# Experts' stage: best 16 sought among 64 sums, marks in fp16, one-hots in one pass, dots paced beside U, one return a tile

## Chip, cores and metric

The kernel runs on one core of a Trainium2 chip. The metric is the device time of one execution in microseconds. Five engines work side by side and are synchronised by semaphores only: TensorE (PE, with its weight loads as PEld), VectorE (DVE), ScalarE (ACT), GpSimd (POOL) and SyncE (SP), which here does nothing but issue DMAs. Each runs its own instructions strictly in order.

## What is computed

A first block (attention, a state-space layer, and a mixture of experts with product keys), then two hybrid layers with feed-forward parts, over 512 tokens of width 1024 in fp32. The change touches the mixture of experts alone:

```python
q = (hc @ w_query).reshape(T, 8, 256)                        # 8 heads
s1 = einsum('chd,hkd->chk', q[..., :128], keys1)             # 128 keys a half
s2 = einsum('chd,hkd->chk', q[..., 128:], keys2)
v1, i1 = top_k(s1, 16);  v2, i2 = top_k(s2, 16)
cand = (v1[..., :, None] + v2[..., None, :]).reshape(T, 8, 256)
sc, ci = top_k(cand, 16)
idx = take(i1, ci // 16) * 128 + take(i2, ci % 16)           # one of 16384 experts
g = softmax(sc)
act = gelu(einsum('chkd,cd->chk', peer_u[idx], hc)) * g
out = einsum('chk,chkd->cd', act, peer_v[idx])
```

## The kernel before

The 512 tokens are four tiles of 128, one token a partition. Tiles 0 to 2 (384 tokens) are computed densely: all 16384 experts, 128 U tiles of 128 experts each, then 128 V tiles; the gates, mostly zero, decide what counts. Tile 3 (`GATHERED`) is computed by gathering: 128 picks (8 heads x 16), for each one row of U and one of V per token, 512 KB a pick.

Each fp32 weight tile (512 KB) is loaded into one of three raw buffers, rounded by ScalarE to fp32r (L338) and its remainder taken by VectorE (L348, "split"); three products (L357 to L359, high x high, high x low, low x high) make one fp32 product. `split_ve` and `split_ac` run up to four tiles ahead of TensorE.

- `pe_u`, `ac_u`, `ve_u`, `sp_u` go through 144 items: 16 query tiles `("wq", c)` and 128 `("U", j)`. A U item is 24 matmuls of 384 columns; ScalarE takes the Gelu of the result (L2021) into one of three buffers, and SP stores it to DRAM (`sp_act`, "acts", 192 KB).
- Beside them, VectorE picks: `ve_top` (best 16 of 128), `ve_cand` (the 16 x 16 sums of a head), `ve_best` (best 16 of 256, five operations of `ve_top16`), `ve_places` (row and column from the place), `ve_mark` (looks up the index by a comparison with 0..15, a product and a sum), `ve_index` (rows to gather). Then `ve_gate`: for 8 tokens at a time, one-hot matrices of both indices in fp16, the second times the gate as two fp16 parts; TensorE multiplies them (`pe_gate`, 16 matmuls of 128 columns), ScalarE copies the result out, and each four groups SP stores 2 MB of gates.
- GpSimd gathers with an indirect DMA (L2081), first the 128 rows of U, then those of V, into five row buffers in turn. `ve_dot` (L2152) multiplies and sums a U row, `ve_row` (L2175) adds a weighted V row to one of two accumulators.
- In V, step j is 18 matmuls of 512 columns into six banks held to the end (`pe_v`). Its left side is acts x gates: SP brings back acts (`sp_back`, 192 KB a tile, six buffers) and gates (`sp_gc`, 768 KB for four tiles, pieces of 512 bytes), VectorE multiplies (L2324), ScalarE rounds (AH, L2316), VectorE takes the remainder (AL, L2326): `ve_prep`/`ac_prep`, `LEAD` = 3 tiles ahead of TensorE.
- The last four V tiles (`TAIL`) are done token tile by token tile, so that the next stage's norm can start: before tile i's last product TensorE does the turn (transpose) of a finished tile, `self.next.pe_turn(order[i])`, and order is 3, 0, 1, 2.

The order is written out by `Peer.schedule`: it goes through the items with a time budget for VectorE (4.4 us for a query item, 3.0 for a U item, 0.8 more with a gate) and puts in units with assumed costs until it is used up; dots fill what is left from four items after the index is known. `later` does the same for V with 1.78 us a step. At the end of U, at item `loads0`, SP issues both first gate returns and the first six acts in one batch.

Of the kernel before, what the change touches and what calls it, by code (L numbers as in the profile page):

```python
# [1824 lines left out]
class Peer:  # L1825
    def __init__(self, k):
# [6 lines left out]
        self.I1T, self.I2T = ar(TOKENS, dt=HF), ar(TOKENS, dt=HF)  # L1833
        self.GP = ar(2, TOKENS, dt=HF)
# [7 lines left out]
        self.IOI = ar(16).bitcast(I32)  # L1842
        self.IOF = ar(16)
        self.KT = ar(16, 128)
        self.V12 = ar(4, 8, 2, 16)
        self.IX = ar(4, 8, 2, 16)
        self.SC, self.CI, self.CJ = ar(4, 8, 16), ar(4, 8, 16), ar(4, 8, 16)
        self.IXu, self.CIu, self.CJu = (x.bitcast(U32) for x in (self.IX, self.CI, self.CJ))
# [7 lines left out]
        self.MK = ar(8, 16, 16)  # L1856
        self.CA = self.KT.rearrange("p a b -> p (a b)").rearrange("p (h k) -> p h k", k=256)
# [5 lines left out]
        self.O1 = [ar(4, 128, 2, dt=HF) for _ in range(4)]  # L1863
        self.O2 = ar(4, 128, 2, dt=HF)
        self.RH = [ar(2, 4, 128, 2, dt=HF) for _ in range(4)]
# [9 lines left out]
    ROWS, SCORES, CHUNK = 5, 8, 32  # L1875
# [5 lines left out]
    def schedule(self):  # L1881
        units = [("top", c, i) for c in range(16) for i in range(4)] + [("rows",)]
        for i in (GATHERED, 0, 1, 2):
# [5 lines left out]
        cost = {"top": 1.7, "rows": 1.3, "cand": 2.5, "best": 2.4, "places": 2.5, "soft": 0.8, "mark": 7.0,  # L1889
                "index": 0.3, "norm": 2.1, "turned": 3.5, "gate": 2.9, "dot": 1.3}  # L1890
        self.items = [("wq", c) for c in range(16)] + [("U", j) for j in range(128)]
        self.units = [[] for _ in self.items]
        self.extras = [[] for _ in range(len(self.items) + 1)]
        time, turn, known, dots = 0.0, None, None, 0
        for n, (kind, c) in enumerate(self.items):
            time = min(time, 2.0) + (4.4 if kind == "wq" else 3.0)
            while time > 0:
                u = units[0] if units else ("dot", dots)
                wait = u[0] == "top" and n < u[1] + 2 or u[0] == "turned" and n < turn + 2
                if wait or u[0] == "gate" and self.units[n] and ("gate", u[1] - 1) in self.units[n]:  # L1900
                    u = ("dot", dots)
                if u[0] == "dot" and (known is None or n < known + 4 or dots == PICKS):
                    break
                time -= cost[u[0]]
                if u[0] == "gate":
                    time += 0.8
                    self.extras[n + 1].append(u)
                if u[0] == "norm":
                    turn = n
                    self.extras[n + 1].append(("turn",))  # L1910
                if u[0] == "soft":
                    self.extras[n].append(u)
                if u[0] == "index":
                    known = n
                if u[0] == "dot":
                    dots += 1
                    if dots % self.CHUNK == 0:
                        self.extras[n + 1].append(("gelu", dots // self.CHUNK - 1))
                    self.units[n].append(u)
                else:  # L1920
                    self.units[n].append(units.pop(0))
        assert not units
        gates = [n for n, x in enumerate(self.extras) if any(u[0] in ("turn", "gate") for u in x)]
        self.loads0 = max(gates) + 4
        assert self.loads0 < len(self.items) - 1, self.loads0


        later = [("dot", x) for x in range(dots, PICKS)] + [("act", c) for c in range(PICKS // self.CHUNK)]
        later += [("row", x) for x in range(PICKS)]
        self.later, self.gelus, time, gelu = [[] for _ in range(128)], [[] for _ in range(128)], 0.0, 0  # L1930
        for j in range(128):
            time = min(time, 1.0) + 1.78
            while later and time > 0:
                u = later[0]
                if u[0] == "act" and u[1] == PICKS // self.CHUNK - 1 and j < gelu + 2:
# [6 lines left out]
        self.later[127] += later  # L1942

# [45 lines left out]
    def pe_gate(self, n, t):  # L1989
# [6 lines left out]
        for c in range(2):  # L1996
            last = pe.e.matmul(self.gate_bank[:, 128 * (t % 4):128 * (t % 4) + 128],
                               self.O1[n % 4][:, t // 2, :, t % 2], self.RH[n % 4][:, c, t // 2, :, t % 2],
# [4 lines left out]
    def ac_u(self):  # L2003
        k, ac, at = self.k, self.k.ac, self.k.at
        a = ac.e.activation
        for n, (kind, c) in enumerate(self.items):
# [16 lines left out]
            for x in self.extras[n]:  # L2023
# [38 lines left out]
    def po_u(self):  # L2062
# [5 lines left out]
        po.after().tensor_copy(self.IOX, bc(self.IO, 2, 2))  # L2068
        g.iota(self.IOI, pattern=[[1, 16]], base=0, channel_multiplier=0).then_inc(*po.up())
        po.after().tensor_copy(self.IOF, self.IOI).then_inc(*po.up("iota"))  # L2070
# [14 lines left out]
    def ve_u(self):  # L2085
# [3 lines left out]
                "gate": self.ve_gate, "rows": self.ve_rows, "index": self.ve_index, "dot": self.ve_dot}  # L2089
# [12 lines left out]
    def ve_cand(self, i):  # L2102
        k, ve, at = self.k, self.k.ve, self.k.at

        ve.wait_ge(*at("ps", 15))
        a = bc(self.V12[:, i, :, 0, :], 3, 16)
        b = bc(self.V12[:, i, :, 1, :], 2, 16)
        ve.after().tensor_tensor(self.CA.rearrange("p h (a b) -> p h a b", b=16), a, b, ALU.add).then_inc(*ve.up())

    def ve_best(self, i, h):  # L2110
        ve_top16(self.k, self.CA[:, h, :], self.SC[:, i, h, :], self.CIu[:, i, h, :],
                 self.TMP).then_inc(*self.k.ve.up())

    def ve_places(self, i):

        k, ve, v, at = self.k, self.k.ve, self.k.ve.e, self.k.at
        ve.wait_ge(*at("iota"))
        ve.after().tensor_copy(self.IX[:, i], self.IXu[:, i]).then_inc(*ve.up())
        v.tensor_scalar(self.CJu[:, i], self.CIu[:, i], 15, None, ALU.bitwise_and).then_inc(*ve.up())
        ve.after().tensor_copy(self.CJ[:, i], self.CJu[:, i])  # L2120
        v.tensor_scalar(self.CIu[:, i], self.CIu[:, i], 4, None, ALU.logical_shift_right).then_inc(*ve.up())
        ve.after().tensor_copy(self.CI[:, i], self.CIu[:, i]).then_inc(*ve.up())

    def ve_mark(self, i, half):

        ve, MK = self.k.ve, self.MK
        sel, dst = ((self.CI, self.E1), (self.CJ, self.E2))[half]
        ve.after().tensor_tensor(MK, bc(sel[:, i, :, :], 3, 16), bc(bc(self.IOF, 1, 16), 1, 8),
                                 ALU.is_equal).then_inc(*ve.up())
        ve.after().tensor_tensor(MK, MK, bc(self.IX[:, i, :, half, :], 2, 16), ALU.mult).then_inc(*ve.up())  # L2130
        ve.after().tensor_reduce(dst[:, i, :, :], MK, AX, ALU.add).then_inc(*ve.up())
# [62 lines left out]
    def ve_turned(self):  # L2194
        k, ve, v, at = self.k, self.k.ve, self.k.ve.e, self.k.at
        GT, GR = (x[:, 0:TOKENS] for x in self.QT)
        for n, dst in enumerate((self.I1T, self.I2T)):
            ve.wait_ge(*at("peT", n))
            v.tensor_copy(dst, k.got("peT", n)[:, 0:TOKENS]).then_inc(*ve.free(("peT", n)))
        ve.wait_ge(*at("peT", 2))  # L2200
        v.tensor_scalar(GT, k.got("peT", 2)[:, 0:TOKENS], GSCALE, None, ALU.mult).then_inc(*ve.free(("peT", 2)))
        ve.after().tensor_copy(self.GP[:, 0, :], GT).then_inc(*ve.up())
        ve.after().tensor_tensor(GR, GT, self.GP[:, 0, :], ALU.subtract).then_inc(*ve.up())
        ve.after().tensor_copy(self.GP[:, 1, :], GR).then_inc(*ve.up())
        k.end("pick", ve)

    def ve_gate(self, n):
        k, ve, v, at = self.k, self.k.ve, self.k.ve.e, self.k.at
        o1, o2, rh = self.O1[n % 4], self.O2, self.RH[n % 4]
        s = slice(8 * n, 8 * n + 8)  # L2210

        def pairs(x):
            return bc(x[:, s].rearrange("p (t u) -> p t u", u=2), 2, 128)

        io = bc(self.IOX, 1, 4)
        if n == 0:
            k.begin(ve, "pick", "ve")
# [9 lines left out]
        last.then_inc(*ve.up("rh", n))  # L2227

    def sp_u(self):
        k, sp, at = self.k, self.k.sp, self.k.at  # L2230
        groups = self.GATES // 4
        for n, item in enumerate(self.items):
# [9 lines left out]
            if n == self.loads0:  # L2242

                sp.wait_ge(*at("gstore", groups - 2))
                sp.wait_ge(*at("gstore", groups - 1))
                sp.wait_ge(*at("pg", self.GATES - 1, 1))
                for c in range(2):
                    self.sp_gc(c)
                for j in range(self.BACK):
                    self.sp_back(j)  # L2250
# [26 lines left out]
    def pe_v(self):  # L2277
        k, pe, at = self.k, self.k.pe, self.k.at
        ps = {(i, n): k.open(2 * i + n, 2 * i + n + 1, "py", i, n) for i in range(DENSE) for n in range(2)}

        def one(j, i, n, w):
            a, c = slice(128 * i, 128 * i + 128), slice(512 * n, 512 * n + 512)
# [3 lines left out]
        for j in range(TAIL):  # L2286
# [3 lines left out]
            for i in range(DENSE):  # L2290
# [37 lines left out]
    def ac_v(self):  # L2328
        k, ac, at = self.k, self.k.ac, self.k.at
        for j in range(self.LEAD):  # L2330
            self.ac_prep(j)
# [11 lines left out]
    def ve_v(self):  # L2343
        k, ve, v, at = self.k, self.k.ve, self.k.ve.e, self.k.at
        does = {"dot": self.ve_dot, "act": self.ve_act, "row": self.ve_row}
        for j in range(self.LEAD):
            self.ve_prep(j)
# [1612 lines left out]
```

## Time and profile before

| | us |
|---|---|
| three runs, median | 4060.3 |
| three runs, lowest and highest | 4057.35, 4067.49 |
| profiled execution, span from first to last instruction | 4053.1 |
| TensorE busy in it | 3751.7 (93%) |
| VectorE busy | 2368.8 (58%) |
| ScalarE busy | 1349.2 (33%) |
| GpSimd busy | 555.0 (14%) |

The page cuts the span into 40 slices of 101 us, in tenths of busy time; the experts' stage is about slices 4 to 17:

```profile
PE   9789999999799999499999788999999999689999
DVE  5746899888688888733237764332333266943332
POOL 8600000111444444300000000000000000100000
PEclk9779999999899999799999879999999999799999
DMA  3003465688999999633322102333222221012222
```

How to read the rows further down. A window's row has start and end, its length, then for each engine busy us and, in brackets, how many instructions; then the granted TensorE clock (1.00 is full speed), the mean busy share of the 16 DMA engines, and GB/s. A row in order of time has its start, its duration, engine, line, operation, what is written and read with shapes, and in square brackets how long the engine was idle before it and what released it. Two instructions of one engine overlap a little: start to start is less than a duration. A group's row has line, engine, operation, forms and count, then busy us and mean ns, then idle time before. A DMA's row ends with KB, where known, and the median us from issue to landing.

### The profile page before, as it was taken

To read this page: it belongs to the slowest core of one execution; us is meant where nothing else is said; L and a number is where in the kernel's file an instruction comes from. 1 tells how busy PE (TensorE), PEld (TensorE's weight loads), DVE (VectorE), ACT (ScalarE), POOL (GpSimd) and SP (SyncE) were. 2 spreads that over 40 slices of the span, in tenths; PEclk is the share of its full clock that TensorE was granted. 3 is DMA by queue.
4 is the path that set the end of the run, shared out by engine and by line. 5 is a ranking of instruction groups with operands and counts; after the bars stand their busy time and mean duration, and the time that the engine had idled before them with its cause. 6 is when DMAs were issued, how large, how long until landed. Compare 5 with 4: busy or idle time off the path is not lost. (4 is left out here: it accounts for less than half of the span.)

```text
span 4053.1 us, 46458 instructions
## 1 busy us (share of the span) xinstructions
PE 3751.7 (93%) x18298; PEld 3094.6 (76%) x18298; DVE 2368.8 (58%) x4034; ACT 1349.2 (33%) x2352; POOL 555.0 (14%) x612
## 2 busy tenths in 40 slices
PE   9789999999799999499999788999999999689999
PEld 7667999988677777378787667887887877467877
DVE  5746899888688888733237764332333266943332
ACT  3354333444233333232233334222322233333221
POOL 8600000111444444300000000000000000100000
PEclk9779999999899999799999879999999999799999
DMA  3003465688999999633322102333222221012222
GB/s 123 11 27 89 126 198 170 237 301 302 348 349 352 347 356 351 242 97 96 98 74 73 44 1 79 94 94 96 81 94 94 95 77 53 19 42 78 95 98 73
DMA packets 273433, 574.70 MB, mean 142 GB/s; under 512 B 19952, under 2 KB 159376, under 8 KB 271552
## 3 DMA queue, kind: packets, MB, share of 16 engines
q1 hardware_dynamic: 236256, 437.42, 33.0%
q0 software_dynamic: 36864, 134.23, 9.1%
q8 instruction: 145, 2.38, 0.2%
q14 instruction: 72, 0.59, 0.0%
q10 hardware_dynamic: 96, 0.08, 0.0%
HBM read 517.92 MB, written 53.74 MB: 141 GB/s over the span
## 5 line engine op out<-in xcount | busy, mean ns | idle before, releaser
L348 DVE TENSOR_TENSOR wlast<-wraw,wlast 128x1024 fp32r<-128x1024 f32 x406 | 494.8, 1224 | 498.1 <-ACT wlast L338 497.5
L357 PE MATMUL ps<-XH,wlast 128*128 128x512 f32 (+2 forms) x1888 | 722.0, 382 | 17.6 <-ACT arena L2021 17.6
L359 PE MATMUL ps<-XH,wlast 128*128 128x512 f32 (+2 forms) x1888 | 706.9, 374 | 0.0
L358 PE MATMUL ps<-XL,wlast 128*128 128x512 f32 (+2 forms) x1888 | 706.8, 374 | 0.0
L338 ACT ACTIVATE wlast<-wraw 128x1024 fp32r<-128x1024 f32 x406 | 425.0, 1052 | 248.4 <-PE ps L359 231.5
L348 DVE TENSOR_TENSOR wtwo<-wraw,wtwo 128x1024 fp32r<-128x1024 f32 x212 | 259.5, 1226 | 302.9 <-ACT wtwo L338 302.5
L357 PEld LDWEIGHTS ps<-XH,wlast 128*128 128x128 f32 x1888 | 357.4, 189 | 77.5 <-ACT arena L2021 18.3
L358 PEld LDWEIGHTS ps<-XL,wlast 128*128 128x128 f32 x1888 | 357.8, 189 | 54.6
L359 PEld LDWEIGHTS ps<-XH,wlast 128*128 128x128 f32 x1888 | 356.8, 189 | 55.5
L357 PE MATMUL ps<-XH,wtwo 128*128 128x512 f32 (+1 forms) x960 | 368.0, 383 | 0.3 <-ACT arena L2021 0.3
L358 PE MATMUL ps<-XL,wtwo 128*128 128x512 f32 (+1 forms) x960 | 361.2, 376 | 0.0
L359 PE MATMUL ps<-XH,wtwo 128*128 128x512 f32 (+1 forms) x960 | 361.2, 376 | 0.0
L2081 POOL DMA_INDIRECT arena<-in_u,arena x128 | 175.1, 1368 | 766.1 <-DVE arena L2152 528.4
L338 ACT ACTIVATE wtwo<-wraw 128x1024 fp32r<-128x1024 f32 x212 | 222.9, 1052 | 160.3 <-PE ps L359 155.8
L357 PE MATMUL ps<-wlast,AH 128*128 128x512 f32 x504 | 202.0, 401 | 31.8 <-DVE AL L2326 31.7
L2081 POOL DMA_INDIRECT arena<-in_v,arena x128 | 190.8, 1490 | 210.2 <-DVE X L2175 98.2
L3096 POOL TENSOR_SCALAR_AFFINE_SELECT arena<-arena 128x128 f32<-128x128 f32 x6 | 3.7, 614 | 1484.3 <-DVE arena L3117 1484.3
L357 PEld LDWEIGHTS ps<-XH,wtwo 128*128 128x128 f32 x960 | 182.4, 190 | 28.8 <-ACT arena L2021 0.7
L358 PEld LDWEIGHTS ps<-XL,wtwo 128*128 128x128 f32 x960 | 182.7, 190 | 28.3
L359 PEld LDWEIGHTS ps<-XH,wtwo 128*128 128x128 f32 x960 | 182.4, 190 | 28.6
L2508 DVE TENSOR_TENSOR arena<-arena,ps 128x512 f32<-128x512 f32 x88 | 60.6, 688 | 245.6 <-PE ps L359 245.6
L2316 ACT ACTIVATE AH<-arena 128x384 fp32r<-128x384 f32 x128 | 67.2, 525 | 398.9 <-DVE arena L2324 398.9
(489 smaller groups left out, 7016.3 us busy)
## 6 DMA issues: line engine op xcount, KB each, us to landing
wraw<-in_ut SPq DMA_DIRECT2D x128, 512.0 KB, 4.2
wraw<-in_v SPq DMA_DIRECT2D x128, 512.0 KB, 6.7
wraw<-in_ffn_gate SPq DMA_DIRECT2D x88, 512.0 KB, 3.5
wraw<-in_ffn_up SPq DMA_DIRECT2D x88, 512.0 KB, 3.5
wraw<-in_ffn_down SPq DMA_DIRECT2D x88, 512.0 KB, 3.5
wraw<-in_w_in SPq DMA_DIRECT2D x58, 512.0 KB, 3.7
acts<-arena SPq DMA_DIRECT2D x128, 192.0 KB, 4.7
gates<-arena SPq DMA_DIRECT2D x12, 2048.0 KB, 10.4
```

The costliest lines, as they stand in the source:

```text
L338: ac.e.activation(W.items[n][7], W.rawof(n), ACT.Copy).then_inc(*ac.up("whi", n))
L348: ve.e.tensor_tensor(W.items[n][8], W.rawof(n), W.items[n][7], ALU.subtract).then_inc(*ve.up("wlo", n))
L357: mm(out, lh, rh, start=start, stop=False)
L358: mm(out, lh, rl, start=False, stop=False)
L359: return mm(out, ll, rh, start=False, stop=stop)
L2081: g.indirect_dma_start(out=self.RB[n % self.ROWS], out_offset=None, in_=tables[n // PICKS], in_offset=bass.IndirectOffsetOnAxis(ap=self.PL ...
L2316: ac.e.activation(self.AH[:, j % 6, :], self.AI[j % 6], ACT.Copy).then_inc(*ac.up("ah", j))
L2508: v.tensor_tensor(s, s, k.got((*id, "up", f)), ALU.mult).then_inc(*ve.free(((*id, "up", f),)))
L3096: po.e.affine_select(out=s, in_=s, compare_op=ALU.is_ge, fill=NEG, base=0, pattern=[[-1, 128]], channel_multiplier=1).then_inc(*po.up("cau ...
```

## The change

- `ve_cand` forms 64 of the 256 sums, in four operations: row 0 with all 16 columns, rows 1 to 3 with 8, rows 4 to 7 with 4, rows 8 to 15 with column 0. All places (a, b) with (a+1)(b+1) at most 16 are among them. `ve_best` searches 64.
- `ve_places` gets row A and column B back from a place in this list, with minima and maxima in fp16, and doubles the indices into pairs (`PAIR`).
- `ve_mark` works in fp16: comparison and product over 2048 elements, then four adds that halve the length instead of one reduction.
- `ve_gate` makes both one-hots in one comparison (2048 elements) and both parts of the gates in one product; three buffers of each instead of four. `ve_turned` lays indices and gates out for that.
- `schedule` has new costs, sets at least one dot an item (`PACE`) from four items after the index is known, spreads the returns as one an item from two items after the last gate, puts the first three `prep`s into the last three U items, and fits what is left evenly into 118 V steps.
- `pe_v` opens the banks as they are first used, takes token tiles in the order 1, 2, 0, and in the tail puts the turn of the gathered tile behind tile 0, with tile 0's own ahead of tile 1's last product.
- Two small constants of GpSimd (`IOI`, `IOF`) go.

Cut to its core:

```diff
-        cost = {"top": 1.7, "rows": 1.3, "cand": 2.5, "best": 2.4, "places": 2.5, "soft": 0.8, "mark": 7.0,
-                "index": 0.3, "norm": 2.1, "turned": 3.5, "gate": 2.9, "dot": 1.3}
+        cost = {"top": 1.7, "rows": 1.3, "cand": 1.0, "best": 1.35, "places": 2.8, "soft": 0.8, "mark": 4.1,
+                "index": 0.3, "norm": 2.1, "turned": 3.5, "gate": 2.5, "dot": 1.35}
...
+            if n > last - self.LEAD:
+                self.units[n].append(("prep", n - last + self.LEAD - 1))
+                self.extras[n].append(("prep", n - last + self.LEAD - 1))
+                time -= 1.2
             while time > 0:
...
+                if known is not None and dots < (n - known - 4) * self.PACE:
+                    u = ("dot", dots)
...
-        self.loads0 = max(gates) + 4
+        back = [("gates", 0)] + [("act", j) for j in range(self.BACK)]
+        back[4:4] = [("gates", 1)]
+        for m, x in enumerate(back):
+            self.returns[min(gates + 2 + m, last)].append(x)
...
+        pace = (first * 1.3 + PICKS * 1.28) / 118
         for j in range(128):
-            time = min(time, 1.0) + 1.78
+            time = min(time, 1.0) + pace
...
     def ve_cand(self, i):
+        ve.after().tensor_tensor(CA[:, :, 0:16], a[:, :, 0:1].broadcast_to([128, 8, 16]), b, ALU.add)
+        v.tensor_tensor(CA[:, :, 16:40].rearrange("p h (a b) -> p h a b", b=8), bc(a[:, :, 1:4], 3, 8),
+                        bc(b[:, :, 0:8], 2, 3), ALU.add)
...
     def ve_mark(self, i, half):
-        ve.after().tensor_reduce(dst[:, i, :, :], MK, AX, ALU.add).then_inc(*ve.up())
+        for n in (8, 4, 2):
+            ve.after().tensor_tensor(MK[:, :, 0:n, :], MK[:, :, 0:n, :], MK[:, :, n:2 * n, :],
+                                     ALU.add).then_inc(*ve.up())
...
     def ve_gate(self, n):
-        v.tensor_tensor(o2, io, pairs(self.I2T), ALU.is_equal).then_inc(*ve.up("o2", n))
-        v.tensor_tensor(o1, io, pairs(self.I1T), ALU.is_equal)
-        ve.wait_ge(*at("o2", n))
-        for c in range(2):
-            last = v.tensor_tensor(rh[:, c], o2, pairs(self.GP[:, c]), ALU.mult)
+        v.tensor_tensor(o.rearrange("p c t i u -> p (c t) i u"), bc(self.IOX, 1, 8), pairs(self.I12),
+                        ALU.is_equal).then_inc(*ve.up("o", n))
+        ve.wait_ge(*at("o", n))
+        v.tensor_tensor(rh.rearrange("p c t i u -> p c t (i u)").rearrange("p c t (i u) -> p c t i u", u=2),
+                        bc(o[:, 1], 1, 2), pairs(self.GP).rearrange("p (c t) i u -> p c t i u", c=2),
+                        ALU.mult).then_inc(*ve.up("rh", n))
...
     def sp_u(self):
-            if n == self.loads0:
+            for x in self.returns[n]:
+                if x == ("gates", 0):
                     sp.wait_ge(*at("gstore", groups - 2))
                     sp.wait_ge(*at("gstore", groups - 1))
...
     def pe_v(self):
-            for i in range(DENSE):
+            for i in (1, 2, 0):
...
-                if j == 127:
+                if j == 127 and i:
+                    if i == 1:
+                        self.next.pe_turn(self.next.order[0])
                     self.next.pe_turn(self.next.order[i])
```

## Rows read from the trace of the kernel before

**Rows 1.** Windows: us, busy (count) of PE PEld DVE ACT POOL; PEclk, DMA, GB/s

```profile
459.00:1040.00 581.00, 579.43 (x3746) 547.87 (x3744) 502.48 (x922) 225.87 (x345) 61.10 (x55) 1.00 0.73 243
1040.00:1072.00 32.00, 10.40 (x50) 9.87 (x48) 15.56 (x25) 5.33 (x8) 15.06 (x10) 0.71 0.92 321
1072.00:1657.00 585.00, 540.99 (x2250) 425.11 (x2250) 475.70 (x621) 185.48 (x254) 267.23 (x173) 0.98 0.98 350
...
1100.00:1130.00 30.00, 30.00 (x131) 24.42 (x130) 25.86 (x42) 10.22 (x14) 15.69 (x10) 1.00 0.97 343
...
1657.00:1704.00 47.00, 3.52 (x17) 3.54 (x17) 34.41 (x33) 5.84 (x13) 22.46 (x21) 0.50 0.75 261
```

**Rows 2.** VectorE in order of time, one V step: start, us, operation, idle before

```profile
1636.26 0.56 DVE L2326 TENSOR_TENSOR AL<-arena,AH 128x384 fp32r<-128x384 f32 x1 [0.59 <-ACT AH L2316]
1636.73 1.28 DVE L2175 SCALAR_TENSOR_TENSOR arena<-arena 128x1024 f32<-128x1024 f32 x1
1637.93 1.22 DVE L348 TENSOR_TENSOR wlast<-wraw,wlast 128x1024 fp32r<-128x1024 f32 x1
1639.06 0.55 DVE L2324 TENSOR_TENSOR arena<-arena 128x384 f32<-128x384 f32 x1
1640.21 0.56 DVE L2326 TENSOR_TENSOR AL<-arena,AH 128x384 fp32r<-128x384 f32 x1 [0.59 <-ACT AH L2316]
```

**Rows 3.** VectorE's waits in V, 1072 to 1657: us, times, longest

```profile
DVE AL L2326 <- ACT AH L2316: 74.5, 126, 0.6
DVE arena L2324 <- DMA arena<-acts: 32.9, 21, 3.1
```

**Rows 4.** VectorE's groups by form, 345 to 1030; the gathers' DMAs, 760 to 1000

```profile
L2152 DVE CUSTOM_DVE_ANT_0 arena<-arena 128x1024 f32<-128x1024 f32 x46 | 55.9, 1221 | 6.9 <-DMA arena<-in_u,arena 6.9
...
L2130 DVE TENSOR_TENSOR arena<-arena 128x2048 f32<-128x2048 f32 x8 | 18.3, 2294 | 0.3
...
L1799 DVE MAX8 arena<-arena 128x8 f32<-128x256 f32 x32 | 13.7, 428 | 1.1
...
L1799 DVE MAX8 arena<-arena 128x8 f32<-128x128 f32 x64 | 18.9, 295 | 3.3
...
L2226 DVE TENSOR_TENSOR arena<-arena 128x1024 f16<-128x1024 f16 x96 | 61.8, 685 | 0.0
...
arena<-in_u,arena POOLq DMA_INDIRECT x31, 5.4
```

**Rows 5.** TensorE in order of time at V's end and the next stage's start

```profile
1656.23 0.63 PE L359 MATMUL ps<-wtwo,AL 128*128 128x512 f32 x1
1700.48 3.75 PE L558 MATMUL ps<-arena,X 128*128 128x128 f32 x16 [43.63 <-DVE arena L590]
...
1726.81 0.77 PE L357 MATMUL ps<-XH,wlast 128*128 128x512 f32 x1
```

**Rows 6.** VectorE in order of time: of the last rows, one and the last

```profile
1668.50 1.29 DVE L2175 SCALAR_TENSOR_TENSOR arena<-arena 128x1024 f32<-128x1024 f32 x1 [2.43 <-DMA arena<-in_v,arena]
...
1695.85 1.28 DVE L2175 SCALAR_TENSOR_TENSOR arena<-arena 128x1024 f32<-128x1024 f32 x1
```

**Rows 7.** ScalarE in order of time: Gelu of U tiles, without and with gates

```profile
563.71 0.49 ACT L2021 ACTIVATE arena<-ps 128x384 f32<-128x384 f32 x1 [2.79 <-PE ps L359]
...
567.95 0.49 ACT L2021 ACTIVATE arena<-ps 128x384 f32<-128x384 f32 x1 [2.80 <-PE ps L359]
...
843.65 0.49 ACT L2021 ACTIVATE arena<-ps 128x384 f32<-128x384 f32 x1 [2.97 <-PE ps L359]
...
849.01 0.49 ACT L2021 ACTIVATE arena<-ps 128x384 f32<-128x384 f32 x1 [2.95 <-PE ps L359]
```

**Rows 8.** Hand-over: SP's DMA queue, ScalarE in order of time, one window

```profile
1034.59 9.91 SPq L2271 DMA_DIRECT2D arena<-acts  x6
...
1056.36 0.49 ACT L2021 ACTIVATE arena<-ps 128x384 f32<-128x384 f32 x1 [19.70 <-DMA acts<-arena]
...
1050.00:1055.00 5.00, 0.00 (x0) 0.00 (x0) 0.00 (x0) 0.00 (x0) 0.00 (x0) 0.50 1.04 400
```

More of the change, by code:

```diff
@@ L1862, in __init__ @@
         self.GS = [ar(128, 32) for _ in range(2)]
-        self.O1 = [ar(4, 128, 2, dt=HF) for _ in range(4)]
-        self.O2 = ar(4, 128, 2, dt=HF)
-        self.RH = [ar(2, 4, 128, 2, dt=HF) for _ in range(4)]
+        self.O = [ar(2, 4, 128, 2, dt=HF) for _ in range(self.AHEAD)]
+        self.RH = [ar(2, 4, 128, 2, dt=HF) for _ in range(self.AHEAD)]
         k.close()
@@ L1888, in schedule @@
         units += [("norm",), ("turned",)] + [("gate", n) for n in range(self.GATES)]
-        cost = {"top": 1.7, "rows": 1.3, "cand": 2.5, "best": 2.4, "places": 2.5, "soft": 0.8, "mark": 7.0,
-                "index": 0.3, "norm": 2.1, "turned": 3.5, "gate": 2.9, "dot": 1.3}
+        cost = {"top": 1.7, "rows": 1.3, "cand": 1.0, "best": 1.35, "places": 2.8, "soft": 0.8, "mark": 4.1,
+                "index": 0.3, "norm": 2.1, "turned": 3.5, "gate": 2.5, "dot": 1.35}
         self.items = [("wq", c) for c in range(16)] + [("U", j) for j in range(128)]
+        last = len(self.items) - 1
         self.units = [[] for _ in self.items]
         self.extras = [[] for _ in range(len(self.items) + 1)]
-        time, turn, known, dots = 0.0, None, None, 0
+        self.returns = [[] for _ in self.items]
+        time, turn, known, dots, gates = 0.0, None, None, 0, None
         for n, (kind, c) in enumerate(self.items):
             time = min(time, 2.0) + (4.4 if kind == "wq" else 3.0)
+            if n > last - self.LEAD:
+                self.units[n].append(("prep", n - last + self.LEAD - 1))
+                self.extras[n].append(("prep", n - last + self.LEAD - 1))
+                time -= 1.2
             while time > 0:
@@ L1907, in schedule @@
                     self.extras[n + 1].append(u)
+                    gates = n + 1
                 if u[0] == "norm":
@@ L1922, in schedule @@
         assert not units
-        gates = [n for n, x in enumerate(self.extras) if any(u[0] in ("turn", "gate") for u in x)]
-        self.loads0 = max(gates) + 4
-        assert self.loads0 < len(self.items) - 1, self.loads0
-        later = [("dot", x) for x in range(dots, PICKS)] + [("act", c) for c in range(PICKS // self.CHUNK)]
+        back = [("gates", 0)] + [("act", j) for j in range(self.BACK)]
+        back[4:4] = [("gates", 1)]
+        for m, x in enumerate(back):
+            self.returns[min(gates + 2 + m, last)].append(x)
+        assert gates + 2 + 3 <= last - self.LEAD, gates
+        later = [("dot", x) for x in range(dots, PICKS)]
+        first = len(later)
+        later += [("act", c) for c in range(PICKS // self.CHUNK)]
         later += [("row", x) for x in range(PICKS)]
+        gelued = dots // self.CHUNK
         self.later, self.gelus, time, gelu = [[] for _ in range(128)], [[] for _ in range(128)], 0.0, 0
+        pace = (first * 1.3 + PICKS * 1.28) / 118
         for j in range(128):
-            time = min(time, 1.0) + 1.78
+            time = min(time, 1.0) + pace
             while later and time > 0:
                 u = later[0]
-                if u[0] == "act" and u[1] == PICKS // self.CHUNK - 1 and j < gelu + 2:
+                if u[0] == "act" and u[1] >= gelued and j < gelu + 2:
                     break
@@ L2088, in ve_u @@
                 "soft": self.ve_soft, "mark": self.ve_mark, "norm": self.ve_norm, "turned": self.ve_turned,
-                "gate": self.ve_gate, "rows": self.ve_rows, "index": self.ve_index, "dot": self.ve_dot}
+                "gate": self.ve_gate, "rows": self.ve_rows, "index": self.ve_index, "dot": self.ve_dot,
+                "prep": self.ve_prep}
         for n, item in enumerate(self.items):
@@ new lines, in ve_places @@
+        ve.after().tensor_scalar(B, A, 8.0, 8.0, ALU.mult, ALU.add)
+        v.tensor_scalar(BASE, A, 4.0, 24.0, ALU.mult, ALU.add).then_inc(*ve.up())
+        ve.after().tensor_tensor(BASE, BASE, B, ALU.min).then_inc(*ve.up())
+        ve.after().scalar_tensor_tensor(BASE, A, 16.0, BASE, ALU.mult, ALU.min).then_inc(*ve.up())
+        ve.after().scalar_tensor_tensor(BASE, A, 48.0, BASE, ALU.add, ALU.min).then_inc(*ve.up())
+        ve.after().tensor_tensor(B, CF, BASE, ALU.subtract).then_inc(*ve.up())
@@ L2131, in ve_mark @@
-        ve.after().tensor_reduce(dst[:, i, :, :], MK, AX, ALU.add).then_inc(*ve.up())
+        M4 = MK.rearrange("p (h q) a u -> p h q (a u)", h=8)
+        ve.after().tensor_tensor(M4, M4, bc(self.PAIR[:, :, half].rearrange("p h a u -> p h (a u)"), 2, 8),
+                                 ALU.mult).then_inc(*ve.up())
+        for n in (8, 4, 2):
+            ve.after().tensor_tensor(MK[:, :, 0:n, :], MK[:, :, 0:n, :], MK[:, :, n:2 * n, :],
+                                     ALU.add).then_inc(*ve.up())
@@ L2133, in ve_index @@
+        ve.after().tensor_tensor(dst[:, i].rearrange("p h k -> p (h k)").rearrange("p (q u) -> p q u", u=2),
+                                 MK[:, :, 0, :], MK[:, :, 1, :], ALU.add).then_inc(*ve.up())
     def ve_index(self):
@@ L2241, in sp_u @@
                         *sp.dma(f"gstore{g % 2}", "gstore", g))
-            if n == self.loads0:
[L2244 to L2250, printed above, removed]
+            for x in self.returns[n]:
+                if x == ("gates", 0):
+                    sp.wait_ge(*at("gstore", groups - 2))
+                    sp.wait_ge(*at("gstore", groups - 1))
+                    sp.wait_ge(*at("pg", self.GATES - 1, 1))
+                if x[0] == "gates":
+                    self.sp_gc(x[1])
+                else:
+                    self.sp_back(x[1])
         self.sp_act(127)
@@ L2278, in pe_v @@
         k, pe, at = self.k, self.k.pe, self.k.at
-        ps = {(i, n): k.open(2 * i + n, 2 * i + n + 1, "py", i, n) for i in range(DENSE) for n in range(2)}
+        ps = {}
         def one(j, i, n, w):
+            if j == 0:
+                ps[i, n] = k.open(2 * i + n, 2 * i + n + 1, "py", i, n)
             a, c = slice(128 * i, 128 * i + 128), slice(512 * n, 512 * n + 512)
```

92 lines of the change are left out of this document (47 added, 45 removed).

## The prediction

> **What bounds the kernel now.** I cut the span into stages first, since only the experts' stage is touched [rows 1]. Beside U (459 to 1040 us) TensorE is busy 579 of 581 us: its bound is TensorE, and VectorE, though 502 us busy, only has to keep up. Then come 32 us with 10 us of matmuls; then V, 585 us for 2250 matmuls of 512 columns at a DMA share of 0.98; then 47 us with almost nothing on TensorE, at a granted clock of 0.5. The next stage's first matmul is at 1726.8 [rows 5].
>
> Second, what V waits for. In VectorE's order of time [rows 2] one V step with one row is 3.95 us from AL to AL: the row 1.20, the split 1.13, the product 0.55, 0.59 of waiting for ScalarE's AH, AL 0.47. Without the row that is 2.75. Over the whole stretch the AH wait is 74.5 us in 126 times, and waits for a DMA add 32.9 us in 21 times, 0.26 a step [rows 3]. The schedule puts 68 dots and 109 rows beside the 128 steps and 19 rows behind them. So V costs VectorE 128 x 2.75 = 352, dots 68 x 1.15 = 78 (a dot is 1.22 busy [rows 4], its neighbour starts 0.07 earlier), rows 128 x 1.20 = 154, and about 43 of DMA waits in V and behind it: 627 us, which is what lies between 2 us before V's first matmul and the end of the last row. VectorE sets V's pace, and DMA waits are a twentieth of it. TensorE alone is a little faster: in 30 us without idle time it issued 131 matmuls [rows 1], one in 0.229, and I use 0.231: 4.16 for a step of 18.
>
> Third, the end. TensorE's last matmul before the gap starts at 1656.2 and the next work, the turn of the gathered tile, at 1700.5 [rows 5]. It stands ahead of tile 0's last product in TensorE's queue and waits for the rows, of which the last starts at 1695.9; the last 21 gathers' intervals take 27.4 us from the row at 1668.5 [rows 6].
>
> **The change, part by part.**
>
> *Picking, on VectorE beside U.* It lies beside TensorE, where a U step is 4.24 us, or 5.36 with a gate [rows 7]. Best 16: five operations on 64 sums instead of 256. Rows give 428 ns for 256 and 295 for 128 [rows 4], a slope of 67 ns per 64, so 3 x 67 x 5 = 1.0 us less on each of 32, 33 us. The sums shrink from 2.33 to about 1.0: 5 us. Marks: 24 operations of 2.29 in fp32 become 16 of 2048 in fp16 (1024 take 0.685 [rows 4], so by the fp32 slope halved 1.22) and 32 short adds (0.23 to 0.69): 7.0 to 4.1 on each of 8, 23 us. Places grow from five short operations to fifteen, at 0.19 each from 1.2 to about 2.8: minus 6. Gates: four operations of 1024 fp16, started 0.60 apart, 2.40 together, become two of 2048, 2.35: 2 us. Together 57 us less; the schedule's due times fill them with dots. Counting its lists by hand, 115 dots come to lie beside U instead of 60, 55 x 1.15 = 63 us more, so VectorE's 545 us there face 597 of TensorE, and no lateness exceeds 3.1 us by the counts, against four U tiles of split weights in hand. Worth nothing there: TensorE hides it. The Trainium skill, VectorE: DVE Perf Modes, section on packing two 16-bit values into one read, says this rate of two a cycle needs a step of one in 16-bit data; the doubled layout gives each operand pairs of neighbours, and its tier table has 1224 ns for such an operation of 2048; 0.685 for 1024 [rows 4] agrees. If an operand fell out of it, the second rival below would follow.
>
> *DMA beside U.* With gates a step moves 0.524 MB of U, 0.197 of acts, 0.524 of gates and now 0.524 for one dot: 1.77 MB in 5.36 us, 330 GB/s. V ran at 350 [rows 1] and 5 us of pure backlog at 400 [rows 8], so it fits. A gather lands 5.4 us after issue there [rows 4]; five buffers at a dot a step allow 21 us. GpSimd's and SP's queues gain nothing they'd block on; the three buffers of one-hots instead of four are freed by TensorE a step later, before their next use.
>
> *The hand-over from U to V.* Of its 32 us 50 matmuls need 8.7. The rest comes from SP: two gate returns and six acts go out in one batch, the acts alone take its queue 9.91 us, and ScalarE's Gelu waits 19.7 us for the store of acts queued behind [rows 8]; no Gelu, no free bank, no TensorE. Then three preps before V's first matmul, and slow clock. One return a tile and preps beside U take away 32 - 8.7 = 23, and 1.6 of idle before 1040 [rows 1]: 25 us.
>
> What it puts back: the last 14 U items now move 10.1 MB of loads and acts, 2.1 of the last gates, 2.75 of returns and 24 gathers (29 dots less the five already in), 12.6: 27.5 MB. At 375 GB/s, between the 350 and 400, that is 73 us against 60.5 of TensorE: VectorE, which waits for gathers in order with its splits and preps behind, comes out **13 us late** (8 at 400, 26 at 320). SP also waits for the last gate store, with U loads and act stores behind it; loads run ahead by three raw buffers, and I give 2 us to a late Gelu (0 to 6).
>
> *V.* Banks for tile 0 opened last save under 1 us. Remaining for VectorE: 13 dots and 128 rows by step 118. To there 119 x 2.75 + 13 x 1.15 + 128 x 1.20 = 496 us; TensorE needs 119 x 4.16 = 495. They are level. So V can at best drop from 585 to 2250 x 0.231 = 520: 65 us. But DMA waits remain: 0.26 a step as now would be 31 over 119 steps. By volume, 136 gathers, 119 loads, acts and gates make 179.5 MB, 513 us at 350 GB/s, 17 above 496. I take **28**, near the row per step since the steps get shorter and the returns' slack with them; ends 5 and 65 (320 GB/s). Against this stands VectorE's lead: it preps three tiles ahead, 12.5 us less the 2.5 of the step itself, **10**.
>
> The Trainium skill, DMA: Bandwidth & Descriptors, section on where 436 GB/s comes from, says that HBM binds at about 358 GB/s. Rows disagree for short stretches: 400 over 5 us [rows 8], and the last rows' gathers, 21 x 0.524 MB in 27.4 us, 402 [rows 6]. By the page V's volume takes 501 us, 5 over VectorE's 496, and the late start is 16; by the page alone 16 + 5 - 10 + 2 = 13 would be given back instead of 33, 20 less.
>
> *The end.* The gathered tile's turn moves behind tile 1's first three products, and rows are due by step 118 of 128. The 43.6 us of idle go, with 2 for the turn at low clock and 0.6 for slow matmuls after: 46 us. What was hidden there: nothing but the rows. What is late next is tile 2's norm, 1720.6 to 1726.8, unchanged.
>
> **Sum**, against the profiled execution (span 4053.1; the median 4060.3 is 7.2 above, which I keep): 25 + 65 + 46 = 136 off; back on 13 + 28 - 10 + 2 = 33. Net 103: **3957 us**. Its own range, 3938 to 3980.
>
> **Rivals.**
> A. *TensorE becomes the bound outright*: lateness 5 and waits 5 vanish in the lead of 10. For: fewer gathers a step (1.20 instead of 1.38). Then 136 - 2 = 134: 3926. Chance 0.13.
> B. *Fp16 operations don't run at two a cycle* (a broadcast operand), so the change doesn't do what it says: gates 4.7 instead of 2.35, marks 7. A gate step is 1.2 + 4.7 + 1.15 = 7.05 against 5.36, 48 x 1.7 = 81; marks 24 less 15 slack: 9. Net 103 - 90: 4047. Against: the gates now, with the same pairs, take 0.685 [rows 4]. 0.04.
> C. *DMAs bind*: 320 GB/s through U's tail and V, as gates' returns come in 512-byte pieces: 26 + 65 - 10 + 2 = 83 back, net 53: 4007. For: share 0.98 in V already. Against: 400 for short. 0.19.
> D. *Slower*: dots beside U hold up splits queued behind them on VectorE. Five buffers give five dots in one turnaround of a buffer, from issue over landing to the dot. It bounds steps once it is over five of them, 21 us; some 95 steps with a dot, mean 4.83 us, must each grow by 1.1 to eat 103, which is at a turnaround of 29.6. At 32 a step is 6.4: 95 x 1.57 = 149, net 46 slower: 4106. For: VectorE's queue is strictly in order, and 55 gathers more share the DMA engines with U's weights. Against: issue 0.9 to 1.7 and landing 5.4 [rows 4] leave 12 us unused. 0.03.
>
> Main case 0.61. The 8-in-10 range runs from below A to C, 3922 to 4005. A measurement here tells from no change about 0.3%, 12 us. Faster by more: 0.61 + 0.13 + 0.19 + a half of B = 0.95; within: 0.02; slower: 0.03.
>
> **What would show it.** Beside U TensorE stays busy with steps of 4.24 and 5.36; marks' big operations at 1.2 us, best's near 0.23; 115 dots there. The hand-over has under 10 us of idle. V takes 535 to 560 us, VectorE's AH wait still 0.59 a step, DMA waits 15 to 45 us. No idle of tens of us before the gathered tile's turn. I'm wrong if gathers leave VectorE waiting in the middle of U, if V's DMA waits exceed 60 us, or if U's steps lengthen.

## The result, and the profile after

The changed kernel takes 4012.6 us (median of 4 runs, 4006.5 to 4016.9) against 4060.3 before: ratio 0.9868, 95% interval 0.9843 to 0.9893. That is 48 us faster, outside 0.3%, and less than half of the 103 that the prediction had. Its profiled execution spans 4012.1 us, 41.0 below the 4053.1 of before.

To see where the time went I cut the touched stage at six events that both traces have, and took their starts from the engines' order of time: the Gelu of U tile 0, the Gelu of tile 66 (about where gates begin), the Gelu of tile 117 (where they end), V's first matmul, the last AL, and the next stage's first matmul.

| from, to | before | after | measured | forecast |
|---|---|---|---|---|
| Gelu 0, Gelu 66 | 277.9 | 282.0 | +4.1 | 0 |
| Gelu 66, Gelu 117 | 271.4 | 288.8 | +17.4 | 0 |
| Gelu 117, V's first matmul | 67.4 | 54.4 | -13.0 | -25 +13 +2 = -10 |
| V's first matmul, last AL | 586.3 | 567.2 | -19.0 | -65 +28 -10 = -47 |
| last AL, next stage | 68.4 | 29.7 | -38.7 | -46 |
| sum | 1271.4 | 1222.2 | -49.2 | -103 |

The span fell by 8 less than the sum, since this execution came to Gelu 0 at 463.0 us instead of 455.4. Nothing is explained with that: a second execution of the same changed kernel (e0) came there at 447.8, and those of its variants between 450.1 and 456.7. In what follows this ledger, from Gelu 0 to the next stage, stands beside the medians. Its first two lines are best read together: in the changed kernel the first two gates (32 of the 768 gate matmuls) come ahead of tile 66, in the one before none does, and the steps of 4.24 us without gates are unchanged.

The same windows as [rows 1], cut at these events, of the changed kernel (us; busy and count of PE, PEld, DVE, ACT, POOL; PEclk, DMA share, GB/s):

```profile
745.00:1034.00 289.00, 272.51 (x1967) 239.20 (x1965) 233.39 (x253) 119.29 (x198) 88.23 (x56) 1.00 0.88 304
1034.00:1088.00 54.00, 43.73 (x239) 42.94 (x238) 33.23 (x48) 13.35 (x20) 25.10 (x19) 0.91 1.04 397
1088.00:1655.00 567.00, 537.65 (x2253) 428.58 (x2251) 447.05 (x542) 186.89 (x256) 222.31 (x140) 0.98 0.94 332
1655.00:1685.00 30.00, 23.33 (x116) 19.90 (x117) 16.96 (x51) 18.24 (x54) 0.00 (x0) 0.89 0.12 36
```

Read the first: with gates TensorE is busy 272.5 us of 289, where [rows 1] had it busy throughout. VectorE is busy 233 of the 289, so in sum it has time to spare. Read the third: V's DMA share fell from 0.98 to 0.94 and its rate from 350 to 332 GB/s, so the DMA engines were less full in a stage that still fell short of its forecast.

The picking itself came out as costed. VectorE's groups by form, 345 to 1034 us, answering [rows 4] (out<-in, count, busy us, mean ns, idle before):

```profile
L2270 DVE TENSOR_TENSOR arena<-arena 128x2048 f16<-128x2048 f16 x48 | 58.8, 1225 | 1.6
...
L2168 DVE TENSOR_TENSOR arena<-arena 128x2048 f16<-128x2048 f16 x8 | 9.8, 1225 | 0.3
...
L1799 DVE MAX8 arena<-arena 128x8 f32<-128x64 f32 x32 | 7.3, 228 | 1.1
```

Marks and gates take 1.225 us an operation (1.22 forecast), the `MAX8` over 64 takes 228 ns (0.23 forecast), and 112 dots lie beside U instead of 60 (115 forecast). What was foretold of these durations and counts held or nearly so; what was wrong is where the time between the operations goes.

**Beside U.** Gelu with gates came every 5.36 us before [rows 7]. ScalarE in order of time, changed kernel:

```profile
854.01 0.49 ACT L2039 ACTIVATE arena<-ps 128x384 f32<-128x384 f32 x1 [2.99 <-PE ps L359]
860.09 0.49 ACT L2039 ACTIVATE arena<-ps 128x384 f32<-128x384 f32 x1 [3.67 <-PE ps L359]
865.51 0.49 ACT L2039 ACTIVATE arena<-ps 128x384 f32<-128x384 f32 x1 [3.01 <-PE ps L359]
871.59 0.49 ACT L2039 ACTIVATE arena<-ps 128x384 f32<-128x384 f32 x1 [3.66 <-PE ps L359]
```

Steps are 6.08, 5.42 and 6.08 us. TensorE's and its weight load's waits, 459 to 1040 us (us in total, times, longest), and VectorE in order of time for one step:

```profile
PE ps L2014 <- DVE arena L2270: 17.5, 25, 1.8
PEld ps L2014 <- DVE arena L2270: 28.1, 45, 2.1
```

```profile
851.05 1.23 DVE L348 TENSOR_TENSOR wlast<-wraw,wlast 128x1024 fp32r<-128x1024 f32 x1 [1.33 <-ACT wlast L338]
852.20 1.22 DVE L2198 CUSTOM_DVE_ANT_0 arena<-arena 128x1024 f32<-128x1024 f32 x1
853.34 0.08 DVE L2198 DVE_READ_ACCUMULATOR2_ANT arena<- 128x1 f32 x1
853.34 1.22 DVE L2267 TENSOR_TENSOR arena<-arena 128x2048 f16<-128x2048 f16 x1
854.59 1.23 DVE L2270 TENSOR_TENSOR arena<-arena 128x2048 f16<-128x2048 f16 x1
```

The matmuls of the gates (L2014) wait for the second pass over the one-hots (L2270), and the step's dot (L2198) runs ahead of both passes, which so run 1.14 us later than they need. Just before, VectorE had stood idle for 1.33 us. That an engine with slack in sum makes TensorE wait by the order within one item is what e1 tests below. In the kernel before the same group of waits is 0.3 us in total, once.

**In V.** VectorE's waits, 1088 to 1656 us, answering [rows 3]:

```profile
DVE AL L2376 <- ACT AH L2366: 77.1, 127, 2.7
DVE arena L2374 <- DMA arena<-acts: 40.2, 23, 3.9
```

The waits for the returns of acts are 40.2 us where [rows 3] has 32.9 and the prediction 28.

**The end.** No idle time of tens of us is left ahead of the gathered tile's turn; the last row's operation starts 19.6 us before the last AL.

### The profile page after: what moved, and what is told of

Read it like the earlier page. It is cut to its first block and busy times, and to the rows that moved or that the text cites. A ratio compares the mean times of both kernels' runs of the same rounds, so it can differ in the third digit from the quotient of the medians.

```text
span 4012.1 us, 46391 instructions
## 1 busy us (share of the span) xinstructions
PE 3762.7 (94%) x18298; PEld 3106.7 (77%) x18298; DVE 2311.8 (58%) x4014; ACT 1347.9 (34%) x2352; POOL 577.3 (14%) x610
## 5 line engine op out<-in xcount | busy, mean ns | idle before, releaser
L357 PE MATMUL ps<-XH,wlast 128*128 128x512 f32 (+2 forms) x1888 | 721.9, 382 | 10.3 <-ACT arena L2039 10.3
L2099 POOL DMA_INDIRECT arena<-in_u,arena x128 | 188.4, 1472 | 582.0 <-DVE arena L2198 368.5
L2099 POOL DMA_INDIRECT arena<-in_v,arena x128 | 204.9, 1601 | 286.8 <-DVE X L2221 144.0
L358 PEld LDWEIGHTS ps<-XL,wtwo 128*128 128x128 f32 x960 | 182.9, 190 | 28.1
L359 PE MATMUL ps<-wlast,AL 128*128 128x512 f32 x504 | 200.9, 399 | 0.0
```

Of the source, the lines that this page charges most:

```text
L357: mm(out, lh, rh, start=start, stop=False)
L358: mm(out, lh, rl, start=False, stop=False)
L359: return mm(out, ll, rh, start=False, stop=stop)
L2099: g.indirect_dma_start(out=self.RB[n % self.ROWS], out_offset=None, in_=tables[n // PICKS], in_offset=bass.IndirectOffsetOnAxis(ap=self.PL ...
```

## Theories and experiments

The prediction's own step left beside U nothing ("TensorE hides it"), and sized the DMA waits in V by volume and by the waits of before. Against that stood, after the comparison:

- T1, order: the dot ahead of the gates delays TensorE. Rivals: the load, 52 more dots on VectorE and 27 MB more of gathers; three one-hot buffers instead of four.
- T2, SP's queue: in V the return of acts is issued behind a load that waits for a free buffer, so it goes out too late. Rival: the DMA engines are at their limit.
- T3, the store of acts holds the hand-over, by the order of the returns. Rival: the volume of transfers there.

Ratios are to the kernel before, run on the same chip. The table has the ledger of each kernel's profiled execution, in the columns of the ledger above ("before" as there).

| kernel | median us | ratio [95%] | U, no gates | gates | hand-over | V | end | sum |
|---|---|---|---|---|---|---|---|---|
| before | | 1 | 277.9 | 271.4 | 67.4 | 586.3 | 68.4 | 1271.4 |
| changed, again (e0) | 4001.3 | 0.9849 [0.9831, 0.9867] | 282.0 | 288.9 | 54.0 | 566.7 | 28.1 | 1219.7 |
| e1 gate first | 3985.1 | 0.9809 [0.9787, 0.9831] | 280.8 | 269.7 | 55.2 | 561.0 | 29.0 | 1195.7 |
| e3 acts first | 4006.6 | 0.9873 [0.9854, 0.9893] | 282.0 | 288.8 | 53.4 | 562.8 | 29.6 | 1216.7 |
| e4 return first | 3971.4 | 0.9781 [0.9764, 0.9798] | 282.0 | 290.5 | 55.5 | 527.3 | 28.2 | 1183.5 |
| e7 e1 and e4 | 3949.3 | 0.9726 [0.9701, 0.9752] | 280.9 | 269.7 | 54.9 | 528.2 | 28.0 | 1161.8 |
| e8 e7, fewer dots late | 3953.0 | 0.9734 [0.9710, 0.9758] | 280.8 | 269.8 | 43.5 | 537.0 | 27.9 | 1158.9 |
| e5 few dots beside U | 4037.9 | 0.9942 [0.9920, 0.9964] | 277.9 | 271.2 | 52.0 | 626.0 | 29.9 | 1257.0 |
| e6 before, return first | 4029.5 | 0.9925 [0.9898, 0.9952] | 277.9 | 271.4 | 67.8 | 553.5 | 70.1 | 1240.7 |

**The changed kernel again (e0)**, beside the next three on one chip: 4001.3, 11 us less than on the first occasion, with overlapping intervals of the ratios; that is just below both ranges that were expected. Its ledger agrees with the first to 1.6 us in every stage, so the stages can be compared more finely than the medians. The late entry into U did not come again (447.8 instead of 463.0), so it is not the change's doing.

> The changed kernel once more, on the same chip as the next three, as their yardstick. Theory and rival alike: 4007 to 4017 us, ratio to before 0.985 to 0.989. One more question: its profiled execution entered U's first tile 7.6 us later than the one of before, at a lower clock between 100 and 150 us, in code that the change does not touch. If that is chance, this profile need not show it.

**The gates' passes ahead of the dot (e1).**

```
+        for us in self.units:
+            if any(u[0] == "gate" for u in us):
+                us.sort(key=lambda u: u[0] == "dot")
```

> The changed kernel, but in each item that holds a gate the dot stands behind the gate's two operations instead of ahead of them. Work and counts are the same. Theory: TensorE waited 17.5 us itself and its weight loads 28.1 us for the one-hots (45 of 48 gates), because the dot's 1.15 us lie ahead of them in VectorE's queue; U's gate items go back from a mean of 5.8 to 5.36 us, U ends about 22 us earlier, total 3990. Rival 1: three one-hot buffers instead of four are the cause (VectorE waits for TensorE's release): then nothing changes, 4012. Rival 2: DMA load of the extra dots is the cause: nothing changes either.

Measured: 3985.1, 16 us less than e0 (its slowest run, 3990.1, is below the fastest of e0, 3992.7); in the ledger the two stretches of U go from 570.9 to 550.5, 20.4 less. That leaves 1.2 us of the 21.5 that U had grown by. The step, VectorE and then one window of 30 us:

```profile
840.99 1.23 DVE L348 TENSOR_TENSOR wlast<-wraw,wlast 128x1024 fp32r<-128x1024 f32 x1 [0.62 <-ACT wlast L338]
842.14 1.22 DVE L2271 TENSOR_TENSOR arena<-arena 128x2048 f16<-128x2048 f16 x1
843.39 1.23 DVE L2274 TENSOR_TENSOR arena<-arena 128x2048 f16<-128x2048 f16 x1
844.53 1.22 DVE L2202 CUSTOM_DVE_ANT_0 arena<-arena 128x1024 f32<-128x1024 f32 x1
845.67 0.08 DVE L2202 DVE_READ_ACCUMULATOR2_ANT arena<- 128x1 f32 x1
846.38 1.23 DVE L348 TENSOR_TENSOR wtwo<-wraw,wtwo 128x1024 fp32r<-128x1024 f32 x1 [0.62 <-ACT wtwo L338]
```

```profile
838.00:868.00 30.00, 30.00 (x225) 26.33 (x225) 26.19 (x29) 14.47 (x24) 5.20 (x6) 1.00 0.94 344
```

The step is 5.39 us from split to split, and TensorE is busy all the time with 225 matmuls; the changed kernel had 28.34 us and 209 in such a window:

```profile
850.00:880.00 30.00, 28.34 (x209) 24.61 (x207) 24.22 (x26) 13.08 (x22) 8.38 (x5) 1.00 0.86 286
```

Every operation, dot and gather of e0 is still there, and the DMA rate even rose to 344 GB/s. The one-hots still have three buffers. So T1 is shown, and the load and the buffers are excluded. V gained 5.7 us besides. VectorE's waits for returns in V are 35.2 us in e1 and 40.0 in e0, so some 4.8 may lie there; why they differ I didn't resolve.

**Acts ahead of gates among the returns (e3).**

```
-        back = [("gates", 0)] + [("act", j) for j in range(self.BACK)]
-        back[4:4] = [("gates", 1)]
+        back = [("act", j) for j in range(self.BACK)]
+        back[3:3] = [("gates", 0)]
+        back += [("gates", 1)]
```

> The changed kernel, but the returns come as act 0, 1, 2, gates 0, act 3, 4, 5, gates 1, so that SP reaches its wait for the last gate store three items later. Theory: SP's 8.5 us of waiting (1028.7 to 1037.2) with loads and act stores queued behind causes the Gelu waits of 6.1 and 12.4 us; without it V begins some 10 us earlier, total 4002. Rival: the hand-over is short of DMA bandwidth (402 GB/s there), whatever the order: within 3 us of the changed kernel.

Measured: 4006.6 beside 4001.3, with runs that overlap, and a hand-over of 53.4 us beside 54.0. SP's wait for the gate store, 7.6 us in the hand-over of the changed kernel, is gone from it, and still the Gelus wait 37.2 us for stores of acts (32.4 in e0). So the order of the returns isn't what holds the hand-over, and T3 falls. One window over that kernel's hand-over:

```profile
1026.00:1086.00 60.00, 51.37 (x266) 48.80 (x265) 38.21 (x58) 16.84 (x26) 29.12 (x21) 0.94 1.02 390
```

The DMA engines are busy throughout at 390 GB/s.

**The return ahead of the load in V (e4).**

```
         for j in range(128):
-            load(k, ("V", j))
             if j >= 1 and j + self.BACK - 1 < 128:
                 self.sp_back(j + self.BACK - 1)
+            load(k, ("V", j))
```

> The changed kernel, but in each V step SP issues the return of acts ahead of the weight load, not behind it, so that it doesn't stand behind the load's wait for a free raw buffer. Theory: VectorE's DMA waits in V (40.2 us in 23) are returns that were issued too late for their landing of 7 us; they fall to under 15 us, total 3987 to 3992. Rival: they come from the DMA engines being full, so that whatever comes earlier pushes something else back: waits 30 to 50 us in sum, total within 5 us of the changed kernel.

Measured: 3971.4, 30 us less than e0, and V 527.3 instead of 566.7, 39.4 less. VectorE's waits in V, and V's window:

```profile
DVE arena L2374 <- DMA arena<-acts: 1.6, 3, 0.7
```

```profile
1078.00:1605.00 527.00, 523.79 (x2253) 421.12 (x2251) 445.10 (x542) 188.59 (x256) 221.29 (x139) 1.00 1.00 357
```

The waits fell from 40.2 us to 1.6 while the DMA engines moved more in each us: 357 GB/s instead of 332. A limit of the DMA engines would have shown the opposite. TensorE is busy 523.8 of 527 us: it is V's bound now. The total, 3971.4, fell by more than was expected (3987 to 3992, some 20 to 25 us off). SP's DMA queue in V, changed kernel, and two of VectorE's products:

```profile
1306.40 0.68 SPq L326 DMA_DIRECT2D wraw<-in_v  x1
1307.18 0.43 SPq L2317 DMA_DIRECT2D arena<-acts  x1
1310.35 0.33 SPq L326 DMA_DIRECT2D wraw<-in_v  x1
1310.78 0.38 SPq L2317 DMA_DIRECT2D arena<-acts  x1
```

```profile
1310.24 0.55 DVE L2374 TENSOR_TENSOR arena<-arena 128x384 f32<-128x384 f32 x1
1316.46 0.56 DVE L2374 TENSOR_TENSOR arena<-arena 128x384 f32<-128x384 f32 x1 [1.00 <-DMA arena<-acts]
```

Each return goes out 0.4 to 0.8 us behind a load, and the load waits until its raw buffer is free: SP waits 437.9 us of V's 567 for the split that frees one. Pairing the nth return with the nth product (128 of each), a return was issued 8.6 us before its product started (median of 100 in V's middle), before and after the change alike, in e4 12.0. A return lands 7.4 us after issue in the changed kernel and 8.2 in e4 (medians of the DMA issues in V). 8.6 leaves 1.2 us for whatever comes late; 12.0 leaves 3.8.

**Both (e7).** The edits of e1 and e4 together.

> The changed kernel with both edits, the gate ahead of the dot and the return of acts ahead of V's weight load. Theory: both losses are real and lie in different stretches, so they add: U's gate items 270 us instead of 289, V (to the last AL) 527 instead of 567, total 3950 to 3955. Rival: once U is quicker, the hand-over or V's DMA share takes it back: 3965 or more.

Measured: 3949.3. From after's ledger 20.2 us go beside U and 39.0 in V, so the two are additive as expected, and this version beats both kernels: 2.7% (111 us) under the one before, which the changed kernel undercut by 1.3 and 1.5% in its two measurements.

**At most one dot an item at the end of U (e8).** e7 with

```
+                if u[0] == "dot" and not units and u[0] in [x[0] for x in self.units[n]]:
+                    break
```

which puts 99 dots beside U instead of 112.

> As the one with both edits, but behind the last gate no more than one dot an item, so that 100 instead of 115 dots lie beside U and 28 instead of 13 beside V. Theory: the hand-over is short of DMA bandwidth (some 400 GB/s); 15 gathers of 0.524 MB less are 20 us of it, so last gate to V's first matmul falls from 55 to about 44 us; V grows since VectorE's step is 4.34 instead of 4.18: plus 14 to 18 us; total 0 to 8 us above the one with both. Rival: SP's waits and not bandwidth set the hand-over: it stays at 55, total 14 to 20 above.

Measured: 3953.0, no different from e7. But the ledger moved: hand-over 43.5 instead of 54.9, V 537.0 instead of 528.2. Windows of the hand-over in e7 and in e8:

```profile
1007.00:1062.00 55.00, 44.08 (x241) 43.12 (x240) 33.32 (x48) 13.49 (x20) 25.63 (x19) 0.91 1.04 396
```

```profile
1004.70:1048.20 43.50, 42.08 (x240) 41.37 (x240) 23.52 (x32) 15.56 (x23) 9.95 (x10) 1.00 0.99 363
```

So 13 gathers fewer (6.8 MB, 17 us at 396 GB/s) give 11.4 us, and TensorE is busy 42.1 of 43.5. TensorE's wait and the Gelus' wait in these two windows, first e7, then e8:

```profile
PE ps L357 <- ACT arena L2043: 10.9, 3, 9.4
ACT arena L2043 <- DMA acts<-arena: 26.8, 5, 12.4
```

```profile
PE ps L357 <- ACT arena L2045: 1.4, 1, 1.4
ACT arena L2045 <- DMA acts<-arena: 22.3, 7, 6.3
```

TensorE waits for ScalarE's Gelu, and the Gelu for a store of acts to land. The longest such wait falls from 12.4 to 6.3 us, and 9.5 of the 11.4 us are TensorE's wait that goes with it. Volume is what e3 and e8 leave as the cause, but it isn't shown alone: e8 also takes 13 dots from VectorE there (busy 33.3 and 23.5 us), and no run thins the gathers without the dots. V takes nearly all back, 8.8 us where 14 to 18 were expected: VectorE has the dots there, and TensorE's waits for AL rise from 3.4 to 9.6 us.

**The quicker picking with few dots beside U (e5).** Changed kernel with the old costs and pace:

```
-        cost = {"top": 1.7, "rows": 1.3, "cand": 1.0, "best": 1.35, "places": 2.8, ...
+        cost = {"top": 1.7, "rows": 1.3, "cand": 2.5, "best": 2.4, "places": 2.5, ...
-    PACE = 1.0
+    PACE = 0.0
```

> The changed kernel with the shorter picking and its orders, but scheduled with the costs of before and without the one dot an item: 57 dots beside U, 71 beside V. Theory: shorter picking has no worth in itself, the 58 dots that it makes room for have; V (to the last AL) 610 to 625 us, U as before the change (gates 271, since the gate stands first again), hand-over 55, end 29: total about 4025 to 4035. Rival: the picking itself was on the path beside U: then as fast as the changed kernel, 4001.

Measured: 4037.9, 0.6% or 24 us faster than before. The total is 3 us above what was expected and far from the rival's 4001. U costs what it did before (277.9 and 271.2), so the quicker operations in themselves bring nothing there, and the longer U of the changed kernel comes with the dots. The trace has 54 dots beside U and 74 beside V, three more than was expected there, and V becomes 626.0. In the ledger, where 14.4 us of the 24 show, the gain comes from the hand-over (52.0 instead of 67.4) and the end (29.9 instead of 68.4), less 39.7 that V loses.

**The kernel before with the return first (e6).** The edit of e4 in the kernel before.

> The kernel BEFORE with the one edit that SP issues V's return of acts ahead of the weight load. Theory: its DMA waits in V (32.9 us in 21) have the same cause as in the changed kernel; they fall under 5 us and, as VectorE sets its V too, the kernel gets 25 to 32 us faster: 4030 to 4036. Rival: they're the price of a full DMA: waits stay at 25 or more, 4061 within 5.

Measured: 4029.5, 0.75% or some 31 us faster than before. V goes from 586.3 to 553.5, 32.8 less, and [rows 3] had 32.9 us of waits for returns. In e6's V none is left, while the rate rose from 350 to 370 GB/s and a return goes out 12.5 us ahead of its product instead of 8.6. The cause was there before the change.

## Why the prediction was wrong in size

Right were the sign, the bounds read from [rows 1] and [rows 2], the durations, the number of dots within three and the end's mechanism. None of the rivals was what happened: B's slow fp16 didn't show, C's lack of bandwidth came near the measured time (4007) for a wrong reason, since e4 took the waits away at a higher rate, and A's state, TensorE as the outright bound of V, was reached only with e4 and e7.

- *Picking, beside U*: forecast 0, measured +21.5. The step that failed is "Worth nothing there: TensorE hides it". It compared sums, VectorE's 545 us with TensorE's 597 (VectorE's count came out high: it is busy 506 us in the 597 from Gelu 0), and lateness against the split weights in hand. It never asked who else waits for VectorE in an item. The gates' matmuls do, and the dot stood ahead of them (e1: 20.4 back with the work unchanged). Rival D named the right queue but only the splits behind it, and "I'm wrong if U's steps lengthen" was the sign to watch.
- *Hand-over*: forecast 25 off and 15 back, measured 13.0 off: right within 3, but in part by luck. Crowding was foreseen, and 397 GB/s bears it out. But 13 of the 15 were for VectorE coming late with its splits and preps, and only 2 (0 to 6) for a late Gelu. In the changed kernel TensorE waits for the Gelu alone, for 10.3 us:

```profile
PE ps L357 <- ACT arena L2039: 10.3, 2, 9.4
```

- *V*: forecast 520 + 28 - 10 = 538, measured 567.2. e4 parts the 29 us. TensorE's floor is 527.3, not 520: 7. Waits for DMAs were 40.2, not 28: 12. And the lead of 10 gave nothing: with the waits gone V is 39.9 shorter, all of them, so VectorE handed each on to TensorE. The step that failed is that the waits remain: they were taken as given, between a sum by volume (17) and the row of before (31), with the returns' slack named but not sized. The rows showed only a share of 0.98. The cause is the issue behind a waiting load (e4, e6). TensorE's waits for VectorE in V, first the changed kernel, then e4:

```profile
PE ps L357 <- DVE AL L2376: 29.0, 25, 3.1
```

```profile
PE ps L357 <- DVE AL L2376: 2.6, 5, 0.8
```

  Matmuls last longer too where TensorE keeps stopping: busy 537.7 us for 2253 in the changed kernel and 523.8 for as many in e4, at a granted clock of 0.98 and 1.00.
- *The rule on HBM*: the Trainium skill, DMA: Bandwidth & Descriptors, section on where 436 GB/s comes from, has HBM binding at about 358 GB/s. V without waits ran at 357 (e4), which doesn't test it, since TensorE was the bound there. V in e6 at 370, and the hand-overs of 54 to 60 us at 390 to 397, don't agree, and the measurement decides. Of the prediction's own two rows against it, the 400 over 5 us stands; the 402 over the last rows is a miscount: the trace has 18 intervals between rows in these 27.4 us, not 21, and its window from 1668.5 to 1695.85 has 321 GB/s.
- *The end*: forecast 46, measured 38.7. Mechanism right, size off: the gathered tile's turn and tile 0's norm are now exposed. TensorE, changed kernel:

```profile
1661.85 1.95 PE L558 MATMUL ps<-arena,X 128*128 128x128 f32 x16
1666.66 2.72 PE L558 MATMUL ps<-arena,X 128*128 128x128 f32 x16 [2.87 <-DVE arena L590]
1669.04 0.77 PE L357 MATMUL ps<-wtwo,AH 128*128 128x512 f32 x1
```

  2.87 us of idle, slower matmuls behind it (0.77 where full speed has 0.48) and 0.8 us more for the turn make up some 5 of the 7.

With the two orders mended (e7) the time is 3949.3, 8 under the forecast of 3957. The sum's potential was there, and two queues' order kept it; but so near a total is partly luck, since e7 beats the forecast of V by 11 us (528.2 against 539 in the ledger) and misses that of the end by 6.

**Open.** Why e1 shortens V by 5.7 us as well, and e3 by 4; whether the hand-over eases by fewer transfers alone; and where in e8 the balance of dots between the hand-over and V would be best.

## What to carry to other kernels

Busy time compared over a stage says only that an engine can keep up; for each operation put into a queue, list what stands behind it in the same item and which engine waits for that, and put the producer for the bounding engine first. In a queue of DMA issues put those whose buffers are free ahead of one that waits. When a stage shows both a DMA share near 1 and waits for DMAs, compare the time from issue to need with the time to landing before calling it bandwidth.

## What the hardware showed that I had not expected

A DMA share of 1.00 doesn't mean that transfers bind: in V at share 1.00 and 357 GB/s VectorE waited 1.6 us for returns (e4) and at 1.01 and 363 not at all (e8), while at 0.94 and 332 it waited 40.2. The share was also full (1.02 to 1.04) over the hand-overs at 390 to 397 GB/s, for 54 to 60 us, so nearly the same share stands for rates 10% apart. And the stages' lengths repeated to 1.6 us between two executions of one kernel, while the start of the stage moved by 15 us (463.0 and 447.8): here a ledger between events was sharper than the median.
